# One-core hybrid decoder layer: decay gate computed feature-major with one scan instruction, and extra work placed ahead of the weight halves

## What is computed

```python
h = rms_norm(x);  P = h @ w_in                      # r, k, v, lora inputs, attention q k v, pooling, gates
w_log = -softplus(-(w0 + tanh(xw) @ w_up)) - 0.5
decay = exp(-exp(w_log))                            # = exp(-exp(-0.5) * sigmoid(w0 + tanh(xw) @ w_up))
a = sigmoid(a0 + xa @ a_up)
kk = normalised(k * k_k) per head;  k = k * (1 + (a - 1) * k_a)
# per head of 64, over 256 tokens:
#   S = S * decay_t + (S @ -kk_t) (kk_t * a_t)^T + v_t k_t^T ;  o_t = S @ r_t
y_rwkv = (group_norm(o) + bonus) * g
# plus 8 heads of causal attention with ALiBi, a causal pooling mixer,
# x = x + sum(sigmoid(gates) * (y @ w_branch)) @ w_out,  then x + relu(rms_norm(x) @ w_ff1)^2 @ w_ff2
```

## Time and profile before

| | us |
|---|---|
| three runs | 482.10, 482.25, 481.35 (median 482.10) |
| the profiled execution, its time | 481.16 |
| its span, first to last instruction | 479.4 |
| mean granted TensorE clock | 0.993 |

### The profile page before, as it was taken

One profiled execution on the slowest core, in us unless ns is written; L12 is line 12 of the kernel. 1 busy time (PEld: TensorE's weight loads), 2 busy tenths in 40 slices (PEclk: granted clock), 3 DMA queues, 4 the chain that ended last, 5 costly groups with the idle time before them and its releaser, 6 DMA issues.

```text
span 479.4 us, 8761 instructions
## 1 busy us (share of the span) xinstructions
PE 465.2 (97%) x3668; PEld 400.5 (84%) x3668; DVE 296.0 (62%) x405; ACT 248.0 (52%) x378; POOL 32.3 (7%) x41
## 2 busy tenths in 40 slices
PE   8998999999999997999999999999999999999997
PEld 5997987878976775778888888999999999999995
DVE  4666799774554755647678868655555555555542
ACT  6578564646556543655634445744454444444530
POOL 2001100021670000101000000000000000000000
PEclk9998999999999998999999999999999999999999
DMA  7776534444342333225465474656556655665602
GB/s 237 220 234 228 186 111 154 132 137 128 94 133 90 116 124 111 92 89 178 148 216 184 132 227 145 200 176 182 197 192 195 196 181 181 194 197 178 197 23 88
DMA packets 48694, 76.91 MB, mean 160 GB/s; under 512 B 2576, under 2 KB 28944, under 8 KB 48656
## 3 DMA queue, kind: packets, MB, share of 16 engines
q1 hardware_dynamic: 48656, 76.36, 50.2%
HBM read 75.30 MB, written 1.05 MB: 159 GB/s over the span
## 4 chain that ended last, share of the span: by engine, by line
PE 81%; DVE 7%; ACT 5%; DMA 4%; issue 2%; SPq 1%; ACTq 0%; DVEq 0%
PE bank L497 24%; PE bank L499 23%; PE bank L498 23%; DMA stage<-in_w_in 4%; DVE w_lo L1144 3%; ACT w_hi L902 2%; PE bank L638 1%; PE bank L762 1%; PE bank L742 1%; PE bank L626 1%; DVE small L1356 1%; DVE att L1349 1%; DVE xs L1464 1%; PE bank L831 1%; PE bank L795 1%
## 5 line engine op out<-in xcount | busy, mean ns | idle before, releaser
L1144 DVE TENSOR_TENSOR w_lo<-stage,w_hi 128x1024 fp32r<-128x1024 f32 x138 | 168.6, 1227 | 117.6 <-ACT w_hi L902 117.5
L902 ACT CAST w_hi<-stage 128x1024 fp32r<-128x1024 f32 x138 | 144.3, 1050 | 110.6 <-PE bank L499 96.2
L497 PE MATMUL bank<-h_hi,w_hi 128*128 128x256 f32 x384 | 110.5, 288 | 0.3 <-DVE h_lo L1388 0.3
L498 PE MATMUL bank<-h_lo,w_hi 128*128 128x256 f32 x384 | 109.3, 285 | 0.0
L499 PE MATMUL bank<-h_hi,w_lo 128*128 128x256 f32 x384 | 109.2, 284 | 0.0
L497 PEld LDWEIGHTS bank<-h_hi,w_hi 128*128 128x128 f32 x384 | 74.3, 194 | 1.6 <-issue 0.8
L498 PEld LDWEIGHTS bank<-h_lo,w_hi 128*128 128x128 f32 x384 | 74.3, 193 | 0.7
L499 PEld LDWEIGHTS bank<-h_hi,w_lo 128*128 128x128 f32 x384 | 74.2, 193 | 0.0
L497 PE MATMUL bank<-w_hi,h_hi 128*128 128x512 f32 x144 | 61.6, 428 | 0.0
L499 PE MATMUL bank<-w_hi,h_lo 128*128 128x512 f32 x144 | 56.9, 395 | 0.0
L498 PE MATMUL bank<-w_lo,h_hi 128*128 128x512 f32 x144 | 56.8, 395 | 0.0
(11 more groups left out here) (230 smaller groups left out, 546.9 us busy)
## 6 DMA issues: line engine op xcount, KB each, us to landing
stage<-in_w_ff SPq DMA_DIRECT2D x64, 512.0 KB, 3.8
stage<-in_w_in SPq DMA_DIRECT2D x54, 512.0 KB, 3.5
stage<-in_w_branch SPq DMA_DIRECT2D x12, 512.0 KB, 4.7
stage<-in_w_out SPq DMA_DIRECT2D x8, 512.0 KB, 4.0
xs<-in_x SPq DMA_DIRECT2D x2, 512.0 KB, 3.9
out<-xs SPq DMA_DIRECT2D x4, 256.0 KB, 2.1
cst<-in_consts SPq DMA_DIRECT2D x1, 608.0 KB, 5.1
att<-in_w SPq DMA_DIRECT2D x1, 256.0 KB, 5.2
```

The costliest lines, as they stand in the source:

```text
L497: pe.matmul(o, lh, rh, start=first, stop=False)
L498: pe.matmul(o, lh, rl, start=False, stop=False)
L902: nc.scalar.copy(w_hi[:, v % RING], stage[:, v % STAGES]).then_inc(hi_done, 1)
L1144: dve.tensor_tensor(w_lo[:, v % RING], stage[:, v % STAGES], w_hi[:, v % RING].bitcast(F32), ALU.subtract)\
```

## The change

It makes z feature-major: PE multiplies with `w_up` as the weights, so that w0 becomes a bias per partition in ACT's sigmoid, written into segments of 65 columns per chunk of 64 tokens (column 0 of each stays 0). One DVE scan instruction over 1040 columns then sums each segment (a `restart` tile of ones with a zero at each segment's start is the factor). ACT takes the two exponentials of all 1040 columns. The line 663 matmuls, the triangle constant and the w0 broadcast are gone; w0 arrives as 512 single elements. The frames are now chunks of 64, so `e_end` holds a factor for every chunk and the state update of steps 0, 1 and 2 multiplies by it. POOL sets `restart` and the zero columns at the start.

It moves, on ACT: in unit 3 the key square ahead of both halves and the exps ahead of the second half; in units 16, 18, 20, 22 `extra(t, 0)` ahead of the first halves and `extra(t, 1)` ahead of the second; the group norm's square from (19, 3) and (23, 2) to (20, 1) and (23, 3). On DVE: `extra(t, 0)` ahead of the first half and `extra(t, 1)` ahead of the second, in all units; the `Y` work ahead of the attention norm's.

```diff
+CHUNKS, SEG = T // HD, HD + 1
+SQUARE_AT = {(20, 1): 0, (23, 3): 1}
...
-                    sp.dma_start(w0_wide, w0[0].partition_broadcast(P)).then_inc(small_in, 16)
+                    sp.dma_start(w0_col, w0[0].rearrange("(j p) -> p j", p=P), allow_slow_non_contiguous=True).then_inc(small_in, 16)
...
+                            zi = pe.matmul(z[:, ts], lora[0:64, 0, P * j:P * j + P], th[0:64], start=True, stop=True)
+                            ai = pe.matmul(a[:, ts], lora[64:128, 1, P * j:P * j + P], lmix[64:128, 0], start=True, stop=True)
...
-                if (t, p) in ((3, 2), (4, 0)):
-                    c = t - 3
-                    pe.wait_ge(sg_ready, c + 1)
-                            ins = pe.matmul(o[:, 256 * jj:256 * jj + 129], sg[:, c, P * j:P * j + P],
-                                            cst[:, C_CUM:C_CUM + 129], start=True, stop=True)
...
                 if (t, p) == (2, 1):
+                    act.wait_ge(small_in, 64)
+                    act.wait_ge(seg_ready, 2)
+                            ins = nc.scalar.activation(sg[:, :, j, :, 1:SEG], o[:, T * jj:T * jj + T].rearrange("p (c s t) -> p c s t", c=TT, s=2),
+                                                       ACT.Sigmoid, bias=w0_col[:, j:j + 1])
...
-                        nc.scalar.activation(sg[:, i], sg[:, i], ACT.Sigmoid).then_inc(sg_ready, 1)
...
-                if (t, p) == (3, 2):
+                if (t, p) == (3, 1):
                     act.wait_ge(kkraw_ready, 1)
                     nc.scalar.activation(ksq, kkn, ACT.Square).then_inc(ksq_ready, 1)
+                if (t, p) == (3, 2):
+                    act.wait_ge(cum_ready, 1)
+                    nc.scalar.activation(e_up_all, cum_all, ACT.Exp, scale=-DECAY).then_inc(e_ready, 1)
+                    nc.scalar.activation(e_dn_all, cum_all, ACT.Exp, scale=DECAY).then_inc(e_ready, 1)
...
             for t in range(SLOTS):
+                step = (t, 2) in STEP_AT
+                if t == 3:
+                    extra(t, 1)
+                if step:
+                    extra(t, 0)
                 for v in split_places(2 * t):
                     high(v)
-                extra(t, 0)
+                if not step:
+                    extra(t, 0)
                 late = t in (S_OUT - 1, S_FF - 1)
-                if t == 2:
+                if t == 2 or step:
                     extra(t, 1)
+                if t == 3:
+                    extra(t, 2)
...
+            def sum_decay():
+                dve.wait_ge(seg_ready, 2)
+                for i in range(2):
+                    copied(dve, ("z", i))
+                dve.tensor_tensor_scan(cum_all, restart, sg_all, 0.0, ALU.mult, ALU.add).then_inc(cum_ready, 1)
...
-                    if n == 1:
+                    if n:
                         copied(dve, ("dS", n))
...
-                        ins = dve.tensor_tensor(whole, whole, e_end.unsqueeze(2).to_broadcast([P, PAIRS, P]), ALU.mult)
+                        ins = dve.tensor_tensor(whole, whole, e_end[:, n // 2, :, n % 2:n % 2 + 1].to_broadcast([P, PAIRS, P]), ALU.mult)
...
             for t in range(SLOTS):
-                if t == 2:
-                    decay_input()
+                if t == 3:
+                    sum_decay()
+                extra(t, 0)
                 for v in split_places(2 * t):
                     low(v)
-                extra(t, 0)
                 late = t in (S_OUT - 1, S_FF - 1)
-                early = t < S_VA
-                if early:
-                    extra(t, 1)
+                extra(t, 1)
                 for v in () if late else split_places(2 * t + 1):
                     low(v)
-                if not early:
-                    extra(t, 1)
```

More of the change, by code:

```diff
@@ L309, in build_layer @@
         pool_sb = big[:, 5, 0:512].rearrange("p (g d) -> p g d", g=4)
[L310 removed]
+        restart, sg_all, cum_all = (ops[:, PAIRS * CHUNKS * SEG * i:PAIRS * CHUNKS * SEG * (i + 1)] for i in range(3))
+        segs = lambda z: z.rearrange("p (c j s t) -> p c j s t", c=TT, j=PAIRS, t=SEG)
+        sg = segs(sg_all)
         xn = big[:, 4:6]
@@ L1265, in extra @@
                     ins.then_inc(xt_ready, 1)
+                l = level_place(t)
+                if l is not None and p == 0:
+                    for e in range(2):
+                        o = take(dve, ("Y", l, e))
+                        dve.tensor_tensor(y_q[:, e], o[:].rearrange("p (i n) -> p i n", n=HD),
+                                          wide(cst[:, C_LEV + HD * l:C_LEV + HD * l + HD], 8), ALU.mult)\
+                           .then_inc(drained_of(("Y", l, e)), 1)
                 if t + 1 in S_TURN and p in (0, 3):
```

109 lines of the change are left out of this document (42 added, 67 removed).

## The result

| | before | changed |
|---|---|---|
| median of four runs, us | 482.18 (481.35 to 482.45) | 475.95 (474.86 to 476.86) |
| the profiled execution, its time | 481.16 | 474.86 |
| its span | 479.4 | 472.7 |
| mean granted TensorE clock | 0.993 | 0.996 |

A forecast was written before the change was run, and what follows sets the result against it. PE, busy 97% of the span, was taken to bound the kernel. 481.16 - 8.6 + 0.2 = 472.8, say 472.6 for the profiled execution; the runs' median was forecast at 473.5 us, range 469.5 to 478.

The forecast's parts named there:

- part 1: Units 16 to 22 and 11: the moved instructions remove PE waits and a low clock, 8.6 us, from 4 to 9.2.
- part 2: Units 2 to 5: the new gate's early gain is lost again by the key root, net about 0, -1 to +4.7.
- the long wait: Unit 20, ahead of line 795: PE's 2.96 us idle time goes to 0.1, and its clock loss of 1.7 with it.
- take the rest, 5.9 by those rows, as 7.5: PE's waits outside unit 4: 5.9 us by PE's rows, taken as 7.5 since PEld shows 1.8 more for line 795.
- Unit 16 was left with 0.5: Unit 16: ACT's four copies now stand ahead of high half 37, so 0.5 us of wait remains, from 0 to 0.9.
- so the clock should hold: At the key norms PE waits only 0.9 us, so the clock stays full and gives 1.7 us back.
- From there on all moves together: Behind the key root: DVE's work of units 6 and 7 begins when PE ends unit 5 and shifts with it.
- a second low clock: Behind the key root's transposes (old line 681): PE idles 3.2 us there and the clock falls again, costing 1.7 us.
- A: PE's arrival at old line 681 sets the time: 468.8, or 471.8 if only the clock holds; chance 0.12 below 470.5.
- B: Unit 20's wait stays in part, as U's copy stands behind DVE's score chain and group mean: 478.2; chance 0.17.
- C: Low halves come late and PE waits about 2.0 us a unit in units 7 to 14: 489.5; chance 0.03.
- D: Removed matmuls and the earlier square bring nothing since PE stands at the next place: 482; chance 0.03.

The follow-up runs named there:

- square_back: The changed kernel with only the group norm's square back at (19, 3) and (23, 2): 475.62 us, ratio 0.9836.
- scan_mult: The changed kernel with the scan replaced by a plain DVE multiply of the same two tiles, leaving out the running sum: 473.81 us, ratio 0.9807.
- high_first_16: The changed kernel with ACT's four copies in unit 16 behind high half 37 again: 474.69 us, ratio 0.9842.
- all_three: The changed kernel with exponentials behind high half 11, low half 18 behind unit 6's finish and high half 37 first in unit 16: 473.19 us, ratio 0.9809.
- exps_behind: The changed kernel with ACT's two exponentials behind high half 11 instead of ahead of it: 474.63 us in one run.
- gate_only: The changed kernel with the moves of units 7 and up taken back, except the `Y` move; new gate and early order stay: 482.98 us, ratio 0.9987.
- both_chains: The changed kernel with exponentials behind high half 11 and DVE's key-norm maximum ahead of low halves 12 and 13: 474.90 us, ratio 0.9840.
- low18_behind: The changed kernel with low half 18 behind the finish of unit 6 on DVE: 474.44 us, ratio 0.9824.
- exps_first: Kernel before plus moves of units 7 and up, high half 37 first, key square early, table load and exponentials ahead of it: 470.74 us, ratio 0.9754.
- max_first: The changed kernel with DVE's maximum for the key norms ahead of low halves 12 and 13: 475.19 us in one run.

## Why the prediction was right, and where it wasn't

The sign, the range and most of the mechanisms held. The forecast of the profiled execution was 472.6 and it took 474.86, so 2.3 us are missing: 1.0 in part 1, 0.75 in part 2, 0.15 of start-up and 0.4 outside the span. (Part 2 counts as 0 here, as in 472.6. The recorded sum has -0.2 for it and gives 472.8; the 0.2 between the two has no term of its own.)

**Part 1** was forecast at 8.6 and gave 7.6. By the table and the rows between its columns: the first level's product 0.94, the transposes of line 638 at 144.8 us 0.45, unit 16 0.24, unit 18 0.68, unit 20 2.98, its clock 1.47, unit 22 0.86. The mechanism is right in the places that it names, the long wait most of all: U's copy ends at 182.4, line 785 starts at 182.61 without a wait.

```profile
181.97 0.42 DVE L1291 COPY lora<-bank 128x256 f32<-128x256 f32 x1
```

The step that failed is a size, "take the rest, 5.9 by those rows, as 7.5". The net of waits is 6.15 and not 6.9, and 0.45 of it is line 638, which had no term; with the 0.7 left in unit 16 the lines named gave 6.4, so of the 1.6 us added for PEld's rows only 0.5 was there. (8.3 less the 2.5 put to unit 4 is 5.8; 5.9 is the three lines added up.) The other 0.2 are the clock, 1.47 for 1.7. Unit 16 was left with 0.5 and has 0.7. The square, told as a link of the wait in unit 20, is none of weight (square_back).

**Part 2, up to the key root**, came out within 0.2 us. The scan took 2.32 (forecast 2.2, 1.2 to 3.2), the key norms start at 39.48 (39.45) behind a wait of 0.97 (0.9), and the root's chain gives line 671 its start at 53.11 (53.3). POOL's root and ACT's spread as predicted:

```profile
49.07 2.91 POOL L1480 TENSOR_TENSOR small<-small 128x16 f32<-128x16 f32 x1 [41.31 <-DVE small L1193]
```

```profile
52.01 1.04 ACT L939 COPY mat<-small 128x1024 f32<-128x1024 f32 x1 [0.39 <-POOL small L1480]
```

What fell is the clock: "so the clock should hold" at the key norms, and that it falls behind line 671. It fell at 41.16, behind the short wait of 0.97 us and the sixteen two-column matmuls. PE therefore came later to line 671 and waited 1.2 there, not 3.2, with no low clock behind it. These errors don't show up to this point, as it is the root's chain that sets it: PE is 1.7 us ahead of before, forecast 1.5. scan_mult, high_first_16 and all_three show the case as it was forecast (waits of 2.4 to 2.7 ahead of line 671, low clock at 53), and their `vmix` is no later for it: high_first_16 and the changed kernel start line 689 at 69.47 and 69.51.

**"From there on all moves together"** is the step that failed. PE gained 1.7 us at the key root and was 0.9 behind at `vmix`: 2.6 lost. The prediction had seen that DVE is 9.86 of 10 us busy there, and drew from it that DVE's work shifts with PE. But the change had made DVE itself late. ACT's timeline shows the second half of it:

```profile
43.57 1.03 ACT L892 CAST w_hi<-stage 128x1024 fp32r<-128x1024 f32 x1
44.50 0.83 ACT L1070 ACTIVATE big<-bank,small 128x256 f32<-128x256 f32 x2
45.23 1.99 ACT L892 CAST w_hi<-stage 128x1024 fp32r<-128x1024 f32 x2
49.84 1.05 ACT L892 CAST w_hi<-stage 128x1024 fp32r<-128x1024 f32 x1 [2.62 <-DMA stage<-in_w_in]
```

Low halves 10 and 11 on DVE, first in the kernel before and then in the changed one:

```profile
37.64 1.23 DVE L1144 TENSOR_TENSOR w_lo<-stage,w_hi 128x1024 fp32r<-128x1024 f32 x1 [2.29 <-ACT w_hi L902]
...
39.84 1.22 DVE L1144 TENSOR_TENSOR w_lo<-stage,w_hi 128x1024 fp32r<-128x1024 f32 x1
```

```profile
40.35 1.22 DVE L1146 TENSOR_TENSOR w_lo<-stage,w_hi 128x1024 fp32r<-128x1024 f32 x1 [2.06 <-ACT w_hi L892]
44.63 1.23 DVE L1146 TENSOR_TENSOR w_lo<-stage,w_hi 128x1024 fp32r<-128x1024 f32 x1 [3.05 <-ACT w_hi L892]
```

The first half is low half 10, 2.7 us later than before: its high half stands behind the key square, which waits for the scan and for `kkn`, so the stage buffer comes back at 41.57, and in 38 to 42 us the DMAs move nothing at all (share 0.00 above, 0.47 before the change). Then high half 11 (43.57) stands behind the exponentials, its low half is 4.8 us later than before and gives the stage buffer back at 45.86, and only then can SP load piece 14, for which ACT waits 2.62 us at 49.84. This is why a shorter scan (scan_mult) and exponentials behind high half 11 (exps_behind) each give back about 1 us at `vmix`, and neither all of it. Everything on DVE behind it slips: the mix of unit 5 stands at 59.24, 3.7 us behind the end of PE's unit 5 at 55.5. In sum the 1.7 us that the forecast took off for a second low clock were not lost there, and 2.4 us of a wait that it didn't have were. That the two are of like size is luck, and it keeps part 2 within 0.75 us of its forecast.

**The rivals.** A is out: the early gain at the key root is 1.7 and not 4.7. B is out: no wait for U's copy in unit 20. C is right in kind and wrong in size: extra work on DVE does make work late on which PE waits, but in one place (unit 7, 2.4 us), by the mix and not by a low half, and units 8 to 15 lose nothing. D holds for the gate alone (gate_only, 0.9987), not for the moves. Of the signs to look for, the waits for line 795 under 1 us in sum, the full clock at 180 to 190 us and the scan came true; the wait of 2.5 to 3.5 us ahead of line 681 came with 1.2, and without the low clock behind it.

**The forecast of the median** had one more term that no row of the kernel before could give: the time outside the span. It is 1.74 to 1.86 us in all runs of the kernel before and of the kernels with the old gate, and 2.11 to 2.23 in all runs of kernels with the new one, changed kernel included. That 0.4 us belongs to the gate, and its cause wasn't looked for (the new gate has two more semaphores, three more instructions on POOL and the DMA of single elements; which of them, if any, isn't known).

Still open: two of the changed kernel's four runs took 476.8 us at a mean clock of 0.993 where the profiled one has 0.996. A second stretch of low clock behind the wait of line 689 would explain it, as in the profiles of gate_only (at 69.2 us, behind 2.1 us) and both_chains (at 70.8, behind 2.9). A longer one at the key norms would too: in square_back's profile, with a mean of 0.993 as well, it lasted 6.83 us there, from 41.0. Those runs have no trace, so this is only argued, and the mean clock alone doesn't give the time: the fastest run of low18_behind (473.76) has 0.992.

## What to carry to other kernels

An instruction for which the bottleneck engine waits belongs ahead of work that has slack, in an order written by hand; that and nothing else brought the gain here, by moves of whole instructions past one another. After any early gain, ask which engine has no idle time between there and the next point at which the bottleneck waits for it: the gain is kept only as far as that engine's work moves too, and a stage buffer that comes free late makes it start later. A cheaper form of a step (fewer matmuls, a bias for free) was worth nothing here, as it put more work, in a worse place, on such an engine; the idle time of ACT ahead of the key square was worth more than the new gate.

## What the runs showed of the hardware

- **The scan.** 2.32 us for 1040 columns of float32, 2.2 ns a column, where a two-input multiply of the same tiles took 1.23. The Trainium skill, page "DVE: opcode table, instruction layouts, handler registers and perf-mode slots", section "Datapath and trigger behaviour", says that the built-in scan program runs at half throughput; the trace agrees, with a factor of 1.9.
- **The low clock.** Each stretch of it ahead of the last stores lasted 3.41 us in these traces, but for one of 6.83 in square_back, and the length of the wait ahead doesn't settle where it comes: behind 0.97 us ahead of the key norms in the changed kernel, but not behind 1.33 us there in high_first_16 or 1.47 in exps_behind (where it came at 53.5 and 54.2, behind 2.7 and 2.5 us). Its cost depends on what PE meets next: 1.47 us in unit 20 and 1.64 in gate_only behind line 689, with no wait of PE for some time behind it. Ahead of line 689 it cost nothing: the changed kernel and high_first_16, with the stretch in two places, start it at 69.51 and 69.47, and square_back, with twice the stretch and no wait ahead of line 671, starts it no later, counted from the scan's start (34.19 us against 34.57). So a stretch of low clock ahead of a wait was hidden by the wait.
- **The root on POOL.** The same instruction on 128x16 took 2.91 to 3.04 us in twelve kernels and 3.82 in max_first and both_chains, where two low halves on DVE ran beside it in place of about one. Its timing on POOL is rough, and no run separates the cause.
- **512 single elements.** w0's DMA of single elements was feared for; it doesn't stand out as a wait of any engine in the changed kernel's trace.
